# When the first weights of a two-layer mixer are loaded and used: the first head's slabs and the late map pieces moved

## The reference

```python
def adaln(cond, w_ada, b_ada):
    m = jax.nn.silu(cond) @ w_ada + b_ada
    shift, scale, gate = jnp.split(m, 3, axis=-1)
    return shift, scale, gate
# in reference(), for each layer l:
h_p = y_p * (1.0 + sc_c) + sh_c                      # context; latent tokens alike
q, k, v, ga, bg, cg, xin, gb = even_projections(h, w_in)      # layer 0
o_a = attention(q, k, v) * jax.nn.silu(ga)
o_b = jax.nn.silu(gb) * bg * dwconv(cg * xin, conv_w)
out = jnp.concatenate([o_a, o_b], axis=-1) @ w_out
y_p = layernorm(ALPHA * y_p + gt_c * o_p, ln_g[l], ln_b[l])
```

## Time and profile before

| | |
|---|---|
| median of 3 runs | 2648.71 us (2647.02 to 2648.77) |
| profiled execution, its own time | 2646.36 us |
| its span, first to last instruction | 2644.4 us |
| TensorE busy | 2563.0 us, 97% of the span, mean granted clock 0.985 |
| VectorE busy | 1748.2 us, 66% |
| ScalarE busy | 955.1 us, 36% |
| GpSimd busy | 883.6 us, 33% |
| chain that ended last | PE 92%, DVE 3%, DMA 3% |

### The profile page before, as it was taken

The page is one execution under the profiler, slowest core; times in us unless marked ns, Lnnn a source line. Parts: engine busy times, 40 slices in busy tenths (PEclk is TensorE's granted clock), DMA queues, the critical chain, the costliest instruction groups (busy, mean ns, idle before and its releaser), DMA issues.

```text
span 2644.4 us, 40212 instructions
## 1 busy us (share of the span) xinstructions
PE 2563.0 (97%) x14762; PEld 2502.9 (95%) x14762; DVE 1748.2 (66%) x2778; ACT 955.1 (36%) x1251; POOL 883.6 (33%) x584
## 2 busy tenths in 40 slices
PE   4899999999999999999899989999999999999997
PEld 1599999999999999999899989999999999999996
DVE  1456666776676667667542369999999999574213
ACT  0233333333333333334322254433333333463223
POOL 1010000000000000000244466666666766573444
PEclk8899999999999999999899999999999999999998
DMA  9765555555555555554344424444444344563332
GB/s 373 296 210 182 172 185 179 182 198 192 189 173 182 175 184 181 187 170 165 132 143 140 142 94 134 134 134 134 134 134 134 125 132 133 173 210 127 127 128 80
DMA packets 129645, 436.10 MB, mean 165 GB/s; under 512 B 16240, under 2 KB 26736, under 8 KB 129536
## 3 DMA queue, kind: packets, MB, share of 16 engines
q1 hardware_dynamic: 114336, 406.09, 45.7%
q0 software_dynamic: 5408, 12.81, 1.8%
q10 hardware_dynamic: 9792, 15.73, 1.7%
HBM read 423.03 MB, written 15.18 MB: 166 GB/s over the span
## 4 chain that ended last, share of the span: by engine, by line
PE 92%; DVE 3%; DMA 3%; ACT 1%; issue 1%; POOL 0%; SPq 0%; ACTq 0%; DVEq 0%; POOLq 0%
PE bank L471 29%; PE bank L473 29%; PE bank L472 29%; DMA map<-in_w_ada_dram 2%; DVE o_lo L1067 1%; PE bank L584 1%; PE bank L487 1%; DMA raw<-in_w_out_even_dram 1%; DVE w_lo L369 1%; PE bank L566 1%; PE bank L527 0%; PE bank L575 0%; ACT w_hi L661 0%; DVE x L1200 0%; DVE h_lo L906 0%
## 5 line engine op out<-in xcount | busy, mean ns | idle before, releaser
L471 PE MATMUL bank<-h_hi,w_hi 128*128 128x384 f32 x3584 | 1210.3, 338 | 9.4 <-DVE h_lo L906 9.4
L473 PE MATMUL bank<-h_hi,w_lo 128*128 128x384 f32 x3584 | 1199.9, 335 | 0.0
L472 PE MATMUL bank<-h_lo,w_hi 128*128 128x384 f32 x3584 | 1199.5, 335 | 0.0
L661 ACT ACTIVATE w_hi<-raw 128x1024 fp32r<-128x1024 f32 x576 | 596.7, 1057 | 793.8 <-PE bank L473 710.7
L369 POOL TENSOR_TENSOR w_lo<-raw,w_hi 128x1024 fp32r<-128x1024 f32 x247 | 602.8, 2456 | 574.9 <-ACT w_hi L661 572.6
L471 PEld LDWEIGHTS bank<-h_hi,w_hi 128*128 128x128 f32 x3584 | 674.1, 188 | 19.4 <-issue 14.7
L472 PEld LDWEIGHTS bank<-h_lo,w_hi 128*128 128x128 f32 x3584 | 674.2, 188 | 0.7
L473 PEld LDWEIGHTS bank<-h_hi,w_lo 128*128 128x128 f32 x3584 | 673.8, 188 | 0.0
L369 DVE TENSOR_TENSOR w_lo<-raw,w_hi 128x1024 fp32r<-128x1024 f32 x329 | 410.7, 1262 | 388.1 <-ACT w_hi L661 373.4
L1268 DVE SCALAR_TENSOR_TENSOR bank<-up,cw,bank 128x399 f32<-128x399 f32 x896 | 487.0, 627 | 0.0
L471 PE MATMUL bank<-o_hi,w_hi 128*128 128x384 f32 x1024 | 346.4, 338 | 11.6 <-DVE o_lo L1067 11.6
(11 more groups left out here) (151 smaller groups left out, 1371.6 us busy)
## 6 DMA issues: line engine op xcount, KB each, us to landing
raw<-in_w_in_even_dram SPq DMA_DIRECT2D x256, 512.0 KB, 4.1
raw<-in_w_in_odd_dram SPq DMA_DIRECT2D x192, 512.0 KB, 3.4
raw<-in_w_ada_dram SPq DMA_DIRECT2D x120, 512.0 KB, 4.1
map<-in_w_ada_dram SPq DMA_DIRECT2D x64, 512.0 KB, 12.9
raw<-in_w_out_even_dram SPq DMA_DIRECT2D x64, 512.0 KB, 3.7
raw<-in_w_out_odd_dram SPq DMA_DIRECT2D x64, 512.0 KB, 3.3
gates<-sg ACTq DMA_DIRECT2D x32, 192.0 KB, 2.2
lg<-gates ACTq DMA_DIRECT2D x32, 192.0 KB, 3.7
```

Of the source, the lines that this page charges most:

```text
L471: pe.matmul(out, w_hi[slot][:, t, :], hi[:, kk, :], start=(kk == 0), stop=False)
L472: pe.matmul(out, w_hi[slot][:, t, :], lo[:, kk, :], start=False, stop=False)
L473: mm = pe.matmul(out, w_lo[slot][:, t, :], hi[:, kk, :], start=False, stop=last)
L661: act.activation(w_hi[mine][:], raw[slot][:], ACT.Copy).then_inc(hi_ready, 1)
```

## The change

Loads: slabs 0 to 3 now follow map piece 13, slabs 4 to 7 piece 39, slabs 8 and 9 piece 59. ScalarE splits slabs 0 to 3 after tile 3 of `h`, slabs 4 and 5 after tile 7, slabs 6 and 7 after tile 11, and slabs 8 and 9 one at a time between the evictions of the first head. VectorE makes the low parts 0 to 3 after `finish(0)`, 4 and 5 around the row copies of the third group, 6 and 7 around those of the fourth. TensorE takes two units behind each of the pairs 12 to 27, tiles 0 to 3 of slabs 0 to 3 first and then tiles 4 to 7; four units (tiles 0 to 3 of slabs 4, 5 and 6) behind each of the pairs 28, 29 and 30; and after the last turn tiles 0 to 3 of slab 7, then tiles 4 to 7 of slabs 4 to 7 tile by tile. In OUT0 the late product of a pair comes before the low part and the tiles of `o_lo`.

```diff
--- before.py
+++ after.py
@@ -118,9 +118,9 @@
         _order += [_maps.pop(0) for _ in range(BESIDE[_n - 1])]
 FIRST = Phase(None, 1, [at for at in _order if at[0] == "w"])
 EVEN = Phase(FIRST, HEADS, _order, first=1)
-IN_START = 6
 TOP_FREE = EVEN.w(HEADS - 1, 2 * 7 - 1) + 1 + RING
-RAW_IN_START = FIRST.pos["w"][IN_START - 1] + 2
+LOAD_WITH_MAPS = {13: range(0, 4), 39: range(4, 8), 59: range(8, 10)}
+RAW_IN_START = 10
 
 OUT_SLABS = [("w", s, q) for q in range(4) for s in range(4)]
 LATE_CHUNK = HEADS - 1
@@ -413,12 +413,8 @@
 
             for n in range(len(MAPS)):
                 load_map(n)
-                if n == 2 * len(MAPS) // 4 - 1:
-                    for r in range(RING):
-                        load_even(0, r, FIRST)
-                if n == 3 * len(MAPS) // 4 + 5:
-                    for r in range(RING, RAW_IN_START):
-                        load_even(0, r, FIRST)
+                for r in LOAD_WITH_MAPS.get(n, ()):
+                    load_even(0, r, FIRST)
             for r in range(RAW_IN_START, FIRST.nraw):
                 load_even(0, r, FIRST)
             with sp.Fori(1, EVEN.bodies) as i:
@@ -511,12 +507,11 @@
                             turn_rows(j - 1 + a, 1 - a)
                         for k, t in WITH_MAPS.get((j, a, q), ()):
                             ahead(k, t, t + 1)
-            ahead(4, 0, 2)
             turn_rows(GROUPS - 1, 1)
-            ahead(4, 2, 4)
-            ahead(5, 0, 4)
-            ahead(4, 4, 8)
-            ahead(5, 4, 8)
+            ahead(7, 0, 4)
+            for t in range(4, SLAB_K):
+                for k in range(4, 8):
+                    ahead(k, t, t + 1)
             pe.wait_ge(h_ready, KD)
             pe.sem_inc(head_done, 1)
 
@@ -542,7 +537,7 @@
                     slab(EVEN, i, k, h_hi, h_lo)
                     slab(EVEN, i, k + 1, h_hi, h_lo)
 
-                for k in range(IN_START if first else 0, 8):
+                for k in () if first else range(8):
                     slab(EVEN, i, k, h_hi, h_lo)
                 strip(CG_)
 
@@ -671,11 +666,13 @@
             for t in range(KD):
                 act.wait_ge(full_ready, t + 1)
                 act.activation(h_hi[:, t, :], full[t % 2][:], ACT.Copy).then_inc(top_ready, 1)
-                if t == 7:
+                if t == 3:
                     split_high(FIRST, 0, 0)
                     split_high(FIRST, 0, 1)
+                elif t == 7:
+                    split_high(FIRST, 0, 2)
                 elif t == 11:
-                    split_high(FIRST, 0, 2)
+                    split_high(FIRST, 0, 3)
 
             def last_gate(i):
                 act.wait_ge(slab_used, EVEN.used(i, GB_))
@@ -690,11 +687,16 @@
                     last_gate(i - 1)
                     split_high(FIRST if first else EVEN, i, 1)
                     split_high(FIRST if first else EVEN, i, 2)
-                split_high(FIRST if first else EVEN, i, 3)
+                    split_high(EVEN, i, 3)
+                else:
+                    high_half(FIRST, 0, 8)
                 strip_out(V_, vT[:], ACT.Copy)
                 act.wait_ge(kt_free, i + 1)
                 strip_out(K_, kT[:], ACT.Copy)
-                split_high(FIRST if first else EVEN, i, 4)
+                if not first:
+                    split_high(EVEN, i, 4)
+                else:
+                    high_half(FIRST, 0, 9)
                 strip_out(Q_, qT[:], ACT.Copy)
                 strip_out(GA_, o[:, ds(i, 1), :], ACT.Silu)
                 split_high(FIRST if first else EVEN, i, 5)
@@ -979,19 +981,19 @@
 
                 if first:
                     for j in range(GROUPS):
+                        if j == 3:
+                            low_half(dve, FIRST, 0, 6)
                         row_out(j, 0)
-                        row_out(j, 1)
-                        finish(j)
-                        if j == 1:
-                            low_half(dve, FIRST, 0, 0)
-                            low_half(dve, FIRST, 0, 1)
-                            low_half(dve, FIRST, 0, 2)
-                            low_half(dve, FIRST, 0, 3)
                         if j == 2:
                             low_half(dve, FIRST, 0, 4)
+                        elif j == 3:
+                            low_half(dve, FIRST, 0, 7)
+                        row_out(j, 1)
+                        if j == 2:
                             low_half(dve, FIRST, 0, 5)
-                    low_half(dve, FIRST, 0, 6)
-                    low_half(dve, FIRST, 0, 7)
+                        finish(j)
+                        for k in range(4) if j == 0 else ():
+                            low_half(dve, FIRST, 0, k)
                     low_half(dve, FIRST, 0, 8)
                     low_half(dve, FIRST, 0, 9)
                 for n in range(4 if first else 0, 5):
@@ -1097,6 +1099,8 @@
 
                 def body(i, first, last):
                     for pair in range(8):
+                        if not layer and 1 <= pair < 5:
+                            late_product(i, pair - 1)
                         if not (last and pair == 7):
                             split_low(ph, i, pair + 1)
                         if first and layer:
@@ -1104,8 +1108,6 @@
                         elif first:
                             for n in STEPS_OF.get(pair, ()):
                                 advance(n)
-                        if not layer and 1 <= pair < 5:
-                            late_product(i, pair - 1)
                         if not layer and i == ph.bodies - 1 and pair == 6:
                             sum_late()
                         if i == 0 and pair == 5:
@@ -1455,8 +1457,10 @@
             4: range(24, 29), 5: range(29, KE + 3)}
 EVEN_STEPS = 6 + PARTS * 3
 
-_beside = [(j, a, q) for j in (2, 3) for a in range(2) for q in range(0, PARTS, 2)][4:]
-WITH_MAPS = {at: [divmod(n, SLAB_K) for n in range(3 * m, min(3 * m + 3, 4 * SLAB_K))] for m, at in enumerate(_beside)}
+_pairs = [(j, a, q) for j in range(GROUPS) for a in range(2) for q in range(0, PARTS, 2)]
+_units = [(k, t) for t0 in (0, 4) for k in range(4) for t in range(t0, t0 + 4)]
+WITH_MAPS = {_pairs[12 + m]: _units[2 * m:2 * m + 2] for m in range(16)}
+WITH_MAPS.update({_pairs[28 + m]: [(4 + m, t) for t in range(4)] for m in range(3)})
 
 _INS = ["xT", "w_ada", "w_in_even", "w_out_even", "w_in_odd", "w_out_odd", "params", "conf_w", "rpb",
         "cache_k", "cache_v", "mask", "ident"]
```

## The result

| | kernel before | changed kernel |
|---|---|---|
| median of 5 runs each | 2647.02 us (2646.62 to 2648.77) | 2633.9 us (2629.1 to 2635.29) |
| ratio of the two | | 0.9944 (0.9931 to 0.9957) |
| profiled execution, its own time | 2646.36 us | 2629.1 us |
| its span | 2644.4 us | 2627.1 us |

The kernel became 13.1 us faster; 13.8 us was forecast, and 2635 us stands beside 2633.9. (The forecast started from the median of three runs, 2648.7 us; over five it is 2647.02 us, and 13.8 us less than that is 2633.2 us.) The profiled execution of the changed kernel is its fastest of five, 4.8 us under the median, so its trace shows 17.3 us of gain in the span. That is not a detail: why this execution is faster than the others turned out to be the one part of the change that I had not understood.

The account below looks back on a forecast made before the run. TensorE, busy 97%, was taken as the bound, idling 37.0 us for map pieces and 11.6 us for `o_lo`. Opening 3.5 + OUT0 10.3 = 13.8 us off 2648.7 gave 2635 us, range 2628 to 2642.

Parts of the forecast that it names:

- The term of 8.3 us for sixteen units: Opening: sixteen units done beside pairs 12 to 19 while TensorE waits for transfers, 16 x 0.52 = 8.3 us gained.
- The opening's 3.5 us: Opening: net gain from earlier units less later pair 20, clock, row copy and slab 8; 3.5 us, bounds 0 and 7.
- I allow 1.5 us more at the low clock (0.7 lost): Opening, at pair 20: pair 20 and a turn come first, so 1.5 us more at the lower clock, 0.7 us lost.
- OUT0's 10.3 us: First output projection: 16.4 us lost before, less 3.0, 1.2 and 1.9 us still lost; 10.3 us gained, bounds 5 and 14.
- Tile 13: First output projection: this `o_lo` tile still comes late as VectorE stands still beside GpSimd's slab 7 low part; 3.0 us.
- The clock: First output projection: low clock after the first wait costs 0 to 3 us; 1.9 us taken.
- The rule of the exclusive lock: VectorE and GpSimd lock shared ports for whole instructions; late product 1 can be held too, wait 3.5 us, half a us less gain.
- The opening gives nothing: Rival, opening: units only fill time before a transfer-bound point and new waits eat the rest; 10.3 us alone, 2638 us; chance 0.13.
- The clock holds: Rival, opening and OUT0: both low-clock stretches vanish; 7 + 13 us gained, 2629 us; chance 0.11.
- Another wait: Rival, OUT0: `o_lo` still late at slabs 4 and 8, clock falls twice; 8.5 us gained with the opening, 2640 us; chance 0.09.
- nothing moves: Rival, whole kernel: gains cancel against waits at slab 8 and later; 2645 to 2652 us; chance 0.04.
- slower: Rival, bodies 1 to 3: late products wait for pieces and delay low parts; 17 us cost, 2662 us; chance 0.03.

Follow-up runs that it names:

- the spread kernel: Changed kernel with slabs 4 to 7 loaded one at a time after map pieces 41, 45, 49 and 53 instead of all after piece 39; 2633.23 us.
- the early units taken away: Changed kernel with no units beside pairs 12 to 19, four units behind each of pairs 20 to 27 instead; 2644.2 us.

## Why the prediction was right

**Pair 20 and the units.** Forecast 83.8 us and units from about 56 us, all sixteen done; measured 84.14 and 85.27 us, units from 56 us, all done. The term of 8.3 us for sixteen units stands, by its own experiment. The last pair was expected near 118 us and came at 116.3 and 120.0 us. The wait of 4 to 6 us before pair 20, named as a sign, came in only one of the two (5.31 us, against 2.15).

**The opening's 3.5 us.** (The terms as written add up to 3.7.) Near the middle of two kinds: 5.3 us in one trace, 1.6 us in the other (slab 0 at 1247.01 against 1248.64 us), 2.3 us in the medians with the opening alone. The term that was mis-sized is "I allow 1.5 us more at the low clock (0.7 lost)". In the worse kind TensorE stays at 0.50 until 92 us and is 3.7 us behind the better one, 1.1 us of it because pair 20 comes later. Nor did I see that the two parts of my sum pull against each other: "if it rises within 8 us of dense work" I counted as a help to the units, and it also lengthens the idle time before pair 20 (2.0 of the 3.2 us between the two kinds). The small terms were right: slab 8 1.1 forecast, 1.00 measured; row copy 1.1 forecast, a wait of 0.84 us measured. "TensorE, not the transfers, sets the end" fits these executions, which have no wait for a piece behind pair 20; with the clock full the spread kernel was held by the transfers, with waits for pieces until pair 28 at 106.03 us.

**OUT0's 10.3 us.** Measured 12.1 us in the full change and 12.2 us alone. Tile 13: 3.0 forecast, 2.31 and 2.94 us measured. Tiles 22 and 23: 1.2 forecast, 0.98 us measured. The clock: 1.9 forecast; it stayed at 1.00 in both traces of the changed kernel and with the late products alone, and cost some 1.5 us with the early units taken away. So the term that was off most is the clock's. The three terms were 2.8 us too high together, yet only 1.8 us more than forecast came: even at the full clock thirteen slabs take 1.0 us more than 13 x 4.16 us and their waits (58.4 - 54.1 - 3.3), so 16.4 us was 1 us too much to put down to waits and clock. Of the 12.1 us, 7.3 are less waiting (10.6 to 3.3 us, beside slabs 0 to 12), and 4.8 are the low clock that no longer follows the waits. Stretches of 1 us bear that out: TensorE's busy time in each, times what the granted clock lacked to 1.00, adds up to 4.7 us before and to nothing in the changed kernel (1240 to 1330 us).

**Some luck in the sum.** 13.8 us beside 13.1 us is closer than its parts. The opening alone gave 2.3 us where 3.5 was forecast, OUT0 in the traces 12.1 us where 10.3 was, and the two misses go opposite ways. In both the clock behind a wait has the largest share: its term was too small for the opening's worse kind, and in OUT0 it stood for a fall that didn't come.

**The rule of the exclusive lock.** In these rows VectorE's work stands still beside GpSimd's low part for about as long as GpSimd still works. The row on tile 13 above shows it for the subtraction. For the late product, which no row of before showed, the changed kernel has it in body 1 (VectorE, then GpSimd):

```profile
1316.24 3.56 DVE L1163 SCALAR_TENSOR_TENSOR part_late<-raw,cond,part_late 128x512 f32<-128x512 f32 x2
```

```profile
1315.40 3.18 POOL L369 TENSOR_TENSOR w_lo<-raw,w_hi 128x1024 fp32r<-128x1024 f32 x1 [5.14 <-ACT w_hi L656]
```

3.56 us instead of 1.40 us, with 2.34 us of GpSimd's instruction left when it starts (1318.58 - 1316.24). So the Trainium skill (SBUF — State Buffer, section "SBUF: two separate sides") was right on this operation too. The result that I drew from it, a wait of 3.5 us at tile 13, did not come: the late product ends at 1261.34 us, just ahead of GpSimd's start at 1261.60 us. Who comes second stands still: GpSimd itself came 0.2 us behind VectorE's low part (1261.37 us) and took 3.20 instead of 2.40 us, and only then did VectorE's subtraction stand still behind GpSimd. In the changed kernel run again VectorE's low part itself met GpSimd and took 3.27 us, and the wait was 2.94 us.

**The rivals.** "The opening gives nothing" is the nearest to the worse kind of execution (1.6 us): the clock that it named came, at 0.50 until 92 us, beside the waits of 0.84 and 1.00 us that the forecast had too. "The clock holds" was right for OUT0 and wrong for the opening; its opening, the spread kernel shows, is held by transfers: last pair at 116.9 us and slab 0 of OUT0 4.7 us sooner than before, not the 7 us that I gave it. "Another wait" had its waits at slabs 4 and 8 (2.31 and 0.98 us), but not its price, for the clock did not fall; "nothing moves" and "slower" did not come: in bodies 1 to 3 no wait for `o_lo` or a low part is to be found.

## What to carry to other kernels

Where a buffer's release stands behind long work in one engine's queue, look at how often that loop turns against how often its reader wants it: moving one short operation ahead brought 11 us here (12 in the traces) with no instruction less. Price idle time before dense work twice, once as itself and once at the lower clock behind it, and take each price from rows: here the clock was at the lower level behind the waits of 5.3 to 5.7 us before pair 20, and behind waits of 2.3 us in OUT0 in two traces and not in the others. Whether several short waits are better than one long one isn't shown; the kernel with the spread transfers kept its clock, and its time was not clearly better. When one trace and the median of the same kernel differ by 5 us, profile again before explaining the gain.

## What had not been expected of the hardware

A higher clock beside waits went with a longer time behind them: granted 0.78 instead of 0.51 in 72 to 76 us, 5.31 instead of 2.15 us of idle time, then 0.50 for 8 us, and 3.7 us lost at the last pair. But at 41 us it was the other way round, and the better kind had the higher clock. All five traces with this opening fall into these two kinds. The rows show in what order one thing follows another; why the clock rises at 41 us in some executions and not in others isn't settled.

A wait of 2.3 us was followed by the full clock in the changed kernel (1.00 throughout 1255 to 1290 us) and by a lower one in the kernel without the early units (0.94, 0.72). The length of a single wait does not tell it.
